# A mixture-of-experts block: the rows of the next block gathered and turned inside the down pass, the combine cut in two, the next expert's counts read there too

## The chip, the cores and the metric

One core of a Trainium2 chip runs the whole kernel. The metric is the device time of one execution in microseconds (us); lower is better. TensorE multiplies matrices, VectorE (DVE in the profile) and ScalarE (ACT) do elementwise work and empty PSUM, GpSimd (POOL) does a few set-up steps, SyncE (SP) issues nearly all DMA transfers.

## The reference, cut to what matters

A residual block over 256 tokens of width 1024: a mixer sub-layer (attention and a gated MLP), then a sub-layer with 32 experts, of which each token goes to 4. Everything is float32. The change is in the second one:

```python
logits = xt @ w_router + b_router              # 256 x 32
top_v, top_i = lax.top_k(logits, 4)
gates = softmax(top_v)
def expert(x, e):                              # the tokens that chose e
    gu = x @ w_gate_up[e] + b_gate_up[e]       # 1024 -> 2048
    x_glu = minimum(gu[:, :1024], 7.0)
    x_lin = clip(gu[:, 1024:], -7.0, 7.0)
    act = x_glu * sigmoid(1.702 * x_glu) * (x_lin + 1)
    return act @ w_down[e] + b_down[e]         # 1024 -> 1024
out[token] += gate * expert(x, e)[row of token]
```

Every expert has 12 MB of weights (8 MB gate-up, 4 MB down), all 32 are read, 384 MB in all.

## The kernel before, in words

**Stages.** For about the first 240 us the kernel does the mixer sub-layer and the router; the expert loop follows until about 1155 us, then a last combine, a norm and the output.

**Blocks.** The tokens of an expert are cut into blocks of at most 64 (`TB`). A block with at most 32 tokens runs in a *narrow* form (`m` = 32, each matmul 128x256 output, four column tiles), others in the *wide* form (`m` = 64, 128x512 output, two column tiles). In this run there are 37 blocks, 23 narrow and 14 wide, so five experts have two blocks. `tabs` holds, for each place in the order of experts, the number of blocks, the number of wide ones, and the expert. The first four places are experts 0 to 3; the others are ordered by load so that each four have one of the heaviest.

**One block on TensorE** (`block_of`, L1490): gather the block's rows by a matmul of a 0/1 selection `sel` with the normed tokens `h_sb` into PSUM bank `TOKS` (L1503); add the gate-up bias by small matmuls (L1512); turn the gathered rows by transposes (L1518); gate-up matmuls over eight `k` (L1539); combine the block *before* this one into the four output banks `po`, 4 matmuls (L1484); turn the activations in two halves (L1525); turn the gate-weighted selection `selg` (L1552); down matmuls over eight `k` (L1568). Between these, VectorE copies the gathered rows (L1085), does the clamped SwiGLU (L1091 to L1098) and builds `sel` and `selg` for the next block (L1103, L1107); ScalarE copies the turned rows `hgT` (L720), does the sigmoid (L723), copies the turned activations (L727), the turned selection (L730) and the block's result `y_sb` (L733 wide, L737 to L739 narrow). At an expert's start each engine loads that expert's counts from `tabs` into registers (L1580 and L1581 on TensorE, L1125 on VectorE, L714 on ScalarE).

**Transfers.** SP waits and issues them in one order (L453 to L478). The gate-up weights have two slots of 8 MB, each loaded in four parts of 2 MB; the low half of the down weights has two slots of 2 MB; the high half (`dhi`, 2 MB) has only one. During the last block of an expert, SP waits for these signals of TensorE:

```python
sp.wait_ge(s_gfree, total * 3)       # gate-up k = 0, 1 done: load part 0 of the expert after next
sp.wait_ge(s_gfree, total * 3 + 1)   # k = 2, 3 done: part 1
sp.wait_ge(s_dhi_free, total)        # down pass: six of eight k done (n == 5): dhi of the next expert
sp.wait_ge(s_y, total)               # down pass done: its second part, then parts 2, 3 and dlo
```

So between the first of these and the third only 4 MB are issued, and TensorE must come from the start of gate-up to near the end of the down pass.

**The end.** After the loop TensorE combines the last block (signal `s_fin`), ScalarE loads the table for the square root (L751) and squares (L755, L758), VectorE scales with `gain2`, which comes by a last DMA (L481).

## Time and profile before

| | |
|---|---|
| three runs | 1187.77, 1191.23, 1194.48 us; median 1191.23 |
| the profiled execution: time, and span from first to last instruction | 1186.76 us, 1184.5 us |
| busy share of the span | TensorE matmul 87%, weight load 42%, DVE 25%, ACT 15%, POOL 3% |
| DMA | 464.91 MB, mean 392 GB/s over the span |
| mean granted TensorE clock | 0.938 |
| longest waits of SP's queue | 353.8 us for L1568 (62 times), 222.9 us for L1539 (27 times) |

"PE" is TensorE's matmul row and "PEld" its weight loads; a clock of 1.00 is 2.4 GHz and 0.50 is 1.2 GHz. The trace lists each float32 matmul of the program as two (so a gather of 4 is x8, a narrow down pass x64, a wide one x32). Matmuls of different tiles overlap, so their busy times are not additive and the length of a group is read from where it starts and where the next begins. "issue" in the chain of waits is time in which TensorE waited for nothing that the profile shows. The transfer of an expert is issued long before it lands (a gate-up part has a median of 27.7 us from issue to landing), so SP waiting is no loss in itself: a loss is time in which no DMA engine moves anything.

### The profile page before, as it was taken

The numbers are of one execution on the slowest core, as the hardware profiler recorded it, in microseconds if no ns is written. First come the engines' busy times: TensorE is split into PE (matmuls) and PEld (weight loads), VectorE is DVE, ScalarE is ACT, GpSimd is POOL, SyncE is SP. The second block draws the span as 40 slices with busy tenths as digits, with TensorE's granted clock in tenths as the row PEclk, the third lists the DMA queues.
The fourth block names the chain that finished last, engine by engine and source line by source line (L and its number), as shares of the span: only waits on it lengthen the run. The fifth ranks groups of instructions, "written<-read, shape, count | busy, mean of one in ns | idle before, by whom it ended". The sixth has DMA issues, their size and how long they took to land.

```text
span 1184.5 us, 21565 instructions
## 1 busy us (share of the span) xinstructions
PE 1029.1 (87%) x8299; PEld 502.1 (42%) x8301; DVE 294.9 (25%) x813; ACT 179.7 (15%) x453; POOL 31.6 (3%) x54
## 2 busy tenths in 40 slices
PE   4999999977786999899989998999898989696966
PEld 4847887443342343334333433343334333232323
DVE  4636664241110121111211221112112211111112
ACT  3213340221110111101111111111111111010012
POOL 1001002110000000000000000000000000000000
PEclk9999999978897999899989998999899989898988
DMA  9899825989999979999999999999999999999996
GB/s 351 321 385 380 338 103 226 422 347 417 424 426 423 411 307 425 424 425 396 427 424 425 425 425 427 425 415 425 425 428 411 426 425 424 425 427 427 426 424 261
DMA packets 61484, 464.91 MB, mean 392 GB/s; under 512 B 5900, under 2 KB 10060, under 8 KB 28568
## 3 DMA queue, kind: packets, MB, share of 16 engines
q1 hardware_dynamic: 60736, 462.47, 94.6%
q0 software_dynamic: 336, 1.07, 0.3%
q10 hardware_dynamic: 392, 1.09, 0.2%
q8 instruction: 14, 0.23, 0.1%
q14 instruction: 6, 0.05, 0.0%
HBM read 462.50 MB, written 2.11 MB: 392 GB/s over the span
## 4 chain that ended last, share of the span: by engine, by line
PE 64%; DMA 23%; DVE 5%; issue 4%; ACT 2%; SPq 2%; DVEq 0%; POOL 0%; ACTq 0%
PE pp L1539 23%; DMA arena<-in_w_down_dram 20%; PE pp L1568 13%; PE pp L1325 5%; PE pp L1503 5%; PE pp L1247 2%; PE pp L1338 2%; PE po L1400 2%; PE pp L1257 2%; PE pp L1512 2%; PE po L1484 2%; DMA gain<-gain_dram 2%; DMA arena<-in_w_ada_dram 1%; PE pp L1518 1%; ACT work L720 1%
## 5 line engine op out<-in xcount | busy, mean ns | idle before, releaser
L1539 PE MATMUL pp<-arena,work 128*32 128x256 f32 (+1 forms) x3840 | 379.0, 449 | 20.1 <-ACT work L720 20.1
L1539 PEld LDWEIGHTS pp<-arena,work 128*32 128x32 f32 (+1 forms) x3840 | 168.3, 118 | 214.9 <-issue 131.3
L1568 PE MATMUL pp<-arena,work 128*32 128x256 f32 (+1 forms) x1920 | 200.2, 462 | 54.6 <-DMA arena<-in_w_down_dram 54.6
L1568 PEld LDWEIGHTS pp<-arena,work 128*32 128x32 f32 (+1 forms) x1920 | 77.1, 122 | 157.3 <-issue 67.9
L1091 DVE TENSOR_SCALAR work<-pp 128x128 f32<-128x128 f32 (+1 forms) x74 | 25.0, 338 | 410.2 <-PE pp L1539 410.2
L1503 PE MATMUL pp<-h_sb,work 128*32 128x256 f32 (+1 forms) x480 | 70.0, 514 | 41.9 <-issue 37.5
L723 ACT ACTIVATE work<-work 128x128 f32<-128x128 f32 (+1 forms) x74 | 25.9, 350 | 407.9 <-DVE work L1091 407.9
L1085 DVE COPY work<-pp 128x256 f32<-128x256 f32 (+1 forms) x37 | 19.5, 526 | 250.0 <-PE pp L1503 250.0
L1484 PE MATMUL po<-work 64*128 64x512 f32 x304 | 75.5, 615 | 1.2 <-ACT work L739 1.2
L1503 PEld LDWEIGHTS pp<-h_sb,work 128*32 128x32 f32 (+1 forms) x480 | 22.5, 129 | 84.9 <-issue 79.5
L1325 PE MATMUL pp<-arena 128*128 128x256 f32 x256 | 57.1, 382 | 0.0
L804 DVE SCALAR_TENSOR_TENSOR h_sb<-arena,small,h_sb 128x1024 f32<-128x1024 f32 x38 | 49.5, 1303 | 11.5 <-DMA arena<-in_w_ada_dram 10.3
L1325 PEld LDWEIGHTS pp<-arena 128*128 128x128 f32 x256 | 48.1, 190 | 8.1 <-issue 1.8
L1247 PE MATMUL pp<-arena 128*128 128x256 f32 x192 | 43.7, 390 | 0.3 <-DVE small L865 0.3
L1484 PEld LDWEIGHTS po<-work 64*128 64x128 f32 x304 | 26.2, 186 | 41.0 <-issue 39.2
L1247 PEld LDWEIGHTS pp<-arena 128*128 128x128 f32 x192 | 37.5, 196 | 6.2 <-issue 0.5
L1103 DVE TENSOR_SCALAR work<-iota,rank 128x64 f32 x74 | 15.5, 252 | 96.2 <-issue 91.3
L1107 DVE TENSOR_SCALAR work<-iota,rank,gate_tab 128x64 f32 x148 | 36.2, 309 | 0.0
L720 ACT COPY work<-pp 128x256 f32<-128x256 f32 (+1 forms) x37 | 16.7, 453 | 127.8 <-PE pp L1518 127.8
L1512 PE MATMUL pp<-bgu,pick 4*32 4x256 f32 (+1 forms) x480 | 34.4, 489 | 0.0
L737 ACT COPY work<-pp 128x256 f32<-128x256 f32 x23 | 8.6, 372 | 145.5 <-PE pp L1568 145.5
L1338 PE MATMUL pp<-arena 128*128 128x256 f32 x128 | 28.5, 381 | 0.0
(224 smaller groups left out, 622.7 us busy)
## 6 DMA issues: line engine op xcount, KB each, us to landing
arena<-in_w_gate_up_dram SPq DMA_DIRECT2D x128, 2048.0 KB, 27.7
arena<-in_w_down_dram SPq DMA_DIRECT2D x32, 2048.0 KB, 33.3
arena<-in_w_down_dram SPq DMA_DIRECT2D x64, 1024.0 KB, 20.1
arena<-in_w_ada_dram SPq DMA_DIRECT2D x11, 2048.0 KB, 14.0
arena<-in_w_in_dram SPq DMA_DIRECT2D x4, 2048.0 KB, 19.2
arena<-in_w_gate_dram SPq DMA_DIRECT2D x4, 2048.0 KB, 13.0
arena<-in_w_out_dram SPq DMA_DIRECT2D x2, 2048.0 KB, 10.6
arena<-in_w_ada_dram SPq DMA_DIRECT2D x2, 1024.0 KB, 13.3
```

Of the source, the lines that this page charges most:

```text
L720: a.copy(hgT[:, 0:w], pp[:, TURN, 0:w]).then_inc(s_turned, 1)
L723: a.activation(sig[:, hh, 0:w // 2], glu[:, hh, 0:w // 2], ACT.Sigmoid, scale=ALPHA).then_inc(s_sig, 1)
L804: ins = v.scalar_tensor_tensor(out=acc[:, n % 2, :], in0=page_k(pg, k), scalar=c_act[:, kk:kk + 1], in1=acc[:, n % 2, :], op0=ALU.mult, op ...
L1107: ins = v.tensor_scalar(selg[:, t, c, :], places, rank[:, t, e], gate_tab[:, t, e], ALU.is_equal, ALU.mult)
L1247: mm = t_.matmul(ps[:, i * TOK:(i + 1) * TOK], page_k(pg, k)[:, m * P:(m + 1) * P], hT[:, k, :], start=(k == 0), stop=(k == KD - 1))
L1325: mm = t_.matmul(ps[:, i * TOK:(i + 1) * TOK], page_k(pg, k)[:, m * P:(m + 1) * P], hT[:, k, :], start=(k == 0), stop=(k == KD - 1))
L1338: mm = t_.matmul(branch_bank(m)[:, half * TOK:(half + 1) * TOK], page_k(page_of(name), k)[:, m * P:(m + 1) * P], src[:, k, :], start=(k == 0),
L1484: mm = t_.matmul(po[:, 2 * t + j, :], selgT[j * TB:(j + 1) * TB, t, :], y_sb[j * TB:(j + 1) * TB, :], start=False, stop=last, skip_group_c ...
L1503: mm = t_.matmul(pp[j * m:(j + 1) * m, TOKS, 0:w], sel[:, t, 0:m], h_sb[:, t, j * w:(j + 1) * w], start=(t == 0), stop=(t == TT - 1))
L1512: t_.matmul(pp[j * m:(j + 1) * m, UP[hh], 0:w].rearrange("p (s f) -> p s f", s=2), pick[rows, r, 0:m], bgu[rows, :, cols], start=True, sto ...
L1539: mm = t_.matmul(pp[j * m:(j + 1) * m, UP[hh], 0:w].rearrange("p (s f) -> p s f", s=2), hgT[:, at:at + m], gu_w[slot][:, k, :, r * PAIR:(r ...
L1568: mm = t_.matmul(pp[j * m:(j + 1) * m, UP[0], 0:w], actT[:, at:at + m], wd[:, j * w:(j + 1) * w], start=(n == 0), stop=(n == KD - 1))
```

## The change

The gather of a block's rows (4 matmuls of the wide form, 64 columns of weights and 512 of rows, for narrow blocks too) and their turning move out of the block into the one before: the gather stands in the down pass before its fifth `k` (n == 4), the turning behind its last matmul. For block 1 both stand ahead of the loop. Of the combine's 4 matmuls two are done at the head of the block and two where all four were. The bias matmuls follow the half of the combine. VectorE builds `sel` and `selg` for the next block and copies its gathered rows at the end of each block, with the expert number loaded at the block's start; ScalarE copies the turned rows after `y_sb`. TensorE loads the next place's counts inside the down pass, before the gather. Before the loop VectorE computes `rank` and the first `sel` ahead of the counts. The cut diff:

```diff
@@ ScalarE
+            act.wait_ge(s_turn, 1)
+            a.copy(hgT, pp[:, TURN, :]).then_inc(s_turned, 1)
...
-                    act.wait_ge(s_turn, it)
-                    a.copy(hgT[:, 0:w], pp[:, TURN, 0:w]).then_inc(s_turned, 1)
...
                     if m == TB:
                         a.copy(y_sb, pp[:, UP[0], :]).then_inc(s_ysb, 1)
+                        act.wait_ge(s_turn, it + 1)
+                        a.copy(hgT, pp[:, TURN, :]).then_inc(s_turned, 1)
                         return
...
@@ VectorE
+            first = slice(0, 1)
+            select_rows(iota[:, 0:TB], first)
             counts = pp[:, 2, COUNT:COUNT + NEXP].rearrange("p (e a) -> p e a", a=1).to_broadcast([P, NEXP, 8])
...
+            take_rows(1, UP[1])
+            select_gates(iota[:, 0:TB], first)
...
-                dve.wait_ge(s_hg, it)
-                v.tensor_copy(hg[:, 0:w], pp[:, TOKS, 0:w]).then_inc(s_hgs, 1)
...
-                    dve.wait_ge(s_selT, it)
-                    select(iota[:, bass.ds(b * TB, TB)], e)
+                    past = dve.snap((b + 1) // nb, min_val=0, max_val=1)
+                    next_b = dve.snap((b + 1) % nb, min_val=0, max_val=NBLK - 1)
+                    next_n = dve.snap((past + n) % NEXP, min_val=0, max_val=NEXP - 1)
+                    next_e = dve.value_load(tabs[0:1, 2, bass.ds(next_n, 1)], min_val=0, max_val=NEXP - 1)
                     with dve.If(b < wide):
                         block_of(TB, it, halves)
                     with dve.Else():
                         block_of(NARROW, it, halves)
+                    dve.wait_ge(s_selT, it + 1)
+                    select_rows(iota[:, bass.ds(next_b * TB, TB)], bass.ds(next_e, 1))
+                    select_gates(iota[:, bass.ds(next_b * TB, TB)], bass.ds(next_e, 1))
+                    take_rows(it + 1, TOKS)
...
@@ TensorE
+            def gather(it, bank):
+                pe.wait_ge(s_sel, it)
                 for t in range(TT):
                     for j in range(2):
+                        mm = t_.matmul(pp[j * TB:(j + 1) * TB, bank, :], sel[:, t, :], h_sb[:, t, j * 512:(j + 1) * 512],
+                                       start=(t == 0), stop=(t == TT - 1))
+                mm.then_inc(s_hg, 1)
+
+            def turn_rows(it):
+                pe.wait_ge(s_hgs, it)
+                for i in range(4):
+                    mm = t_.transpose(pp[:, TURN, i * P:(i + 1) * P],
+                                      hg[:, i // 2 * PAIR + i % 2:(i // 2 + 1) * PAIR:2], ident[:])
+                mm.then_inc(s_turn, 1)
+
+            gather(1, UP[1])
+            pe.wait_ge(s_ysb, 2)
+            turn_rows(1)
+            pe.wait_ge(s_bd, 32)
+            pe.wait_ge(s_nblk, 1)
+            pe.wait_ge(s_tabs, 1)
...
                 pe.wait_ge(s_bgu[slot], landed * 2)
-                pe.wait_ge(s_sel, it)
-                for t in range(TT):
+                combine(it, ((0, 0), (0, 1)))
+                for hh in range(2):
                     for j in range(tiles):
-                        if (t, j) == (TT - 1, tiles - 1):
-                            pe.wait_ge(s_ysb, it + 1)
-                        mm = t_.matmul(pp[j * m:(j + 1) * m, TOKS, 0:w], sel[:, t, 0:m],
-                                       h_sb[:, t, j * w:(j + 1) * w], start=(t == 0), stop=(t == TT - 1))
-                mm.then_inc(s_hg, 1)
...
-                pe.wait_ge(s_hgs, it)
-                for i in range(q):
-                    mm = t_.transpose(pp[:, TURN, i * P:(i + 1) * P],
-                                      hg[:, i // 2 * PAIR + i % 2:(i // 2 + 1) * PAIR:2], ident[:])
-                mm.then_inc(s_turn, 1)
...
-                combine(it)
+                combine(it, ((1, 0), (1, 1)))
...
                 for n, k in enumerate(order):
+                    if n == 2:
+                        pe.wait_ge(s_aTev, halves[1])
+                    if n == 4:
+                        next_place()
+                        pe.wait_ge(s_selTev, it)
+                        gather(it + 1, TOKS)
                     if k in (4, 6):
                         pe.wait_ge(s_dhi[k // 2 - 2], dhi_landed)
-                    if n == 2:
-                        pe.wait_ge(s_aTev, halves[1])
-                    if n == KD - 1:
-                        pe.wait_ge(s_selTev, it)
...
                 mm.then_inc(s_y, 1)
+                turn_rows(it + 1)
...
-                    nb = pe.value_load(nblk_i[0:1, bass.ds(i * 2 + slot, 1)], min_val=1, max_val=NBLK)
-                    wide = pe.value_load(wide_i[0:1, bass.ds(i * 2 + slot, 1)], min_val=0, max_val=NBLK)
+                    nb = pe.snap(next_nb, min_val=1, max_val=NBLK)
+                    wide = pe.snap(next_wide, min_val=0, max_val=NBLK)
+
+                    def next_place():
+                        place = pe.snap((i * 2 + (slot + 1)) % NEXP, min_val=0, max_val=NEXP - 1)
+                        pe.reg_mov(next_nb, pe.value_load(nblk_i[0:1, bass.ds(place, 1)], min_val=1, max_val=NBLK))
+                        pe.reg_mov(next_wide, pe.value_load(wide_i[0:1, bass.ds(place, 1)], min_val=0, max_val=NBLK))
```

## Rows read from the trace of the kernel before

**Rows 1.** The page's slices: GB/s moved in each fortieth of the span.
```profile
GB/s 351 321 385 380 338 103 226 422 347 417 424 426 423 411 307 425 424 425 396 427 424 425 425 425 427 425 415 425 425 428 411 426 425 424 425 427 427 426 424 261
```

**Rows 2.** Windows: busy us per engine (PE, PEld, DVE, ACT, POOL), clock, DMA share, GB/s.
```profile
257.00:271.00 14.00, 11.20 (x164) 6.04 (x156) 5.32 (x24) 2.52 (x8) 0.00 (x0) 1.00 0.91 354
419.00:428.00 9.00, 8.84 (x51) 3.43 (x52) 1.96 (x8) 1.47 (x4) 0.00 (x0) 1.00 0.11 27
536.00:549.00 13.00, 11.18 (x164) 6.00 (x160) 3.37 (x14) 2.52 (x8) 0.00 (x0) 1.00 0.94 357
...
248.00:255.00 7.00, 5.77 (x58) 2.23 (x62) 1.73 (x7) 0.37 (x1) 0.00 (x0) 0.50 0.99 411
```

**Rows 3.** Chain of waits: a wide block's down pass, then two narrow blocks.
```profile
640.71 7.02 PE pp L1568 x32
...
650.55 7.51 PE pp L1539 x126
658.05 1.92 PE po L1484 x8
...
661.02 3.59 PE pp L1568 x64
664.62 1.59 issue
...
667.27 0.61 PE pp L1512 x16
...
668.79 3.36 PE pp L1539 x52
```

**Rows 4.** TensorE's sequencer at the down pass's fifth k: count, ns, first and last start.
```profile
L1560 PEldq FUSED_REGOPS  x1: 37/37/37, 661.4 to 661.4; - x1
```

**Rows 5.** TensorE's loads of the first count at one expert's start, the same columns.
```profile
L1580 PEldq TENSOR_LOAD <-tabs x1: 300/300/300, 682.0 to 682.0; - x1
```

**Rows 6.** TensorE's loads of the second count there, the same columns.
```profile
L1581 PEldq TENSOR_LOAD <-tabs x1: 301/301/301, 682.7 to 682.7; - x1
```

**Rows 7.** Timeline: a gather of the wide form.
```profile
684.13 1.94 PE L1503 MATMUL pp<-h_sb,work 128*64 128x512 f32 x8 [1.28 <-issue]
```

**Rows 8.** Timeline: ScalarE's first of three like copies of a narrow block's result.
```profile
664.68 0.37 ACT L737 COPY work<-pp 128x256 f32<-128x256 f32 x1 [3.25 <-PE pp L1568]
```

**Rows 9.** Groups by line and form: ScalarE's copy of 128x512 (busy us, mean ns).
```profile
L733 ACT COPY work<-pp 128x512 f32<-128x512 f32 x14 | 8.2, 585 | 93.4 <-PE pp L1568 93.4
```

**Rows 10.** Chain of waits: between the two wide blocks of one expert.
```profile
392.14 7.02 PE pp L1568 x32
...
400.91 1.02 PE pp L1512 x8
...
403.28 13.12 PE pp L1539 x60
```

**Rows 11.** Chain of waits: from a late DMA landing to the heavy expert's gate-up.
```profile
616.04 1.13 issue
617.17 3.68 PE pp L1503 x8
...
623.51 2.79 PE pp L1539 x11
```

**Rows 12.** Timeline of VectorE before the loop: the gate table.
```profile
243.33 0.39 DVE L1051 TENSOR_SCALAR gate_tab<-work,small 128x32 f32<-128x32 f32 x2
```

**Rows 13.** Timeline of TensorE: block 1's gather and gate-up.
```profile
248.77 1.94 PE L1503 MATMUL pp<-h_sb,work 128*32 128x256 f32 x16 [4.39 <-DVE work L1103]
...
252.84 9.05 PE L1539 MATMUL pp<-arena,work 128*32 128x256 f32 x128 [0.46 <-ACT work L720]
```

**Rows 14.** Timeline of ScalarE at the end: table load, first square.
```profile
1174.23 1.28 ACT L751 ACT_TABLE_LOAD   x1
1175.52 0.60 ACT L755 ACTIVATE h_sb<-po 128x512 f32<-128x512 f32 x1
```

**Rows 15.** Chain of waits at the end: the last DMA before the output.
```profile
1155.11 20.50 DMA gain<-gain_dram
```

More of the change, by code:

```diff
@@ L739, in block_of @@
                     a.copy(y_sb[2 * m:3 * m, w:2 * w], pp[3 * m:P, UP[0], 0:w]).then_inc(s_ysb, 1)
+                    act.wait_ge(s_turn, it + 1)
+                    a.copy(hgT, pp[:, TURN, :]).then_inc(s_turned, 1)
                 with act.Fori(0, nb) as b:
@@ L1098, in block_of, with blocks @@
                     v.tensor_tensor(x_sig, x_lin, x_sig, ALU.mult).then_inc(s_actv, 1)
-            def select(places, e):
-                dve.wait_ge(s_tabs, 1)
-                for t in range(TT):
-                    ins = v.tensor_scalar(sel[:, t, :], places, rank[:, t, e], None, ALU.is_equal)
-                ins.then_inc(s_sel, 1)
-                for t in range(TT):
-                    for c in range(2):
-                        ins = v.tensor_scalar(selg[:, t, c, :], places, rank[:, t, e], gate_tab[:, t, e], ALU.is_equal,
-                                              ALU.mult)
-                ins.then_inc(s_selg, 1)
-            def blocks(nb, wide, e):
+            def blocks(nb, wide, n):
                 with dve.Fori(0, nb) as b:
@@ L1144, in _ @@
             with dve.Fori(1, NEXP) as n:
-                nb, wide, e = place_of(bass.ds(n, 1))
-                blocks(nb, wide, bass.ds(e, 1))
+                nb, wide = place_of(bass.ds(n, 1))
+                blocks(nb, wide, n)
             dve.wait_ge(s_x1b, 16)
@@ L1534, in block_of @@
                             mm.then_inc(s_gfree, 1)
-                    at = (k % q) * P + (k // q) * m
+                    at = (k % 4) * P + (k // 4) * TB
                     for hh in range(2):
@@ L1594, in _ @@
             pe.reg_add(item, item, 1)
-            combine(pe.snap(item, min_val=1, max_val=NEXP * NBLK + 1), last=True)
+            combine(pe.snap(item, min_val=1, max_val=NEXP * NBLK + 1), ((0, 0), (0, 1), (1, 0), (1, 1)), last=True)
 _INS = ["x", "c", "w_ada", "b_ada", "g_pre_mix", "g_post_mix", "w_in", "rel_bias", "sgu_ln_g", "sgu_ln_b",
```

51 lines of the change are left out of this document (31 added, 20 removed).

## The prediction

> **What bounds the kernel now.** I read the slices of the page first. From the tenth slice on nearly all stand at 424 to 428 GB/s [rows 1]: the 384 MB of expert weights are streamed at the full rate, so TensorE's own work costs nothing there. What costs is time in which the DMA engines stand still. I take 427 GB/s as full and read the windows around the slices that fall short [rows 2]. From 257 to 271 us 354 GB/s moved, so 14 x (1 - 354/427) = 2.4 us are lost; from 419 to 428 us 8.4 us; from 536 to 549 us 2.1 us. These two are the first and second expert with two blocks; the others fall into the slices of 415, 411 and 411 GB/s (651, 770 and 888 us on), that is 0.8 to 1.1 us each over 29.6 us [rows 1].
>
> Each of these losses ends when SP is let past the down pass's signal `s_dhi_free`. SP has issued only 4 MB (some 10 us) since the first k of gate-up, and if nothing older is queued the stream dries up until TensorE is six k into the down pass. So of TensorE only two lengths count. One is from the last DMA it waited for to `s_dhi_free` of a heavy expert's last block: five times. The other is the same length in block 1. To these comes the tail behind the last down pass. Whatever is saved or lost in other blocks is covered by the queue.
>
> **Part by part.** All in us; minus is a gain.
>
> *The gather in the down pass.* In a narrow block it took little, but it now has the wide form, 1.94 at full clock [rows 7]. It stands between the halves of the down pass, ahead of `s_dhi_free`: +1.94 in every block. Its inputs are no wait: `sel` needs VectorE about 0.5 behind the turned selection, and half the pass is 1.8 narrow or 3.5 wide [rows 3].
>
> *The counts loaded there.* TensorE's sequencer executes register loads itself, and matmuls behind them wait. One starts at 682.0, the next at 682.7, each 0.3 with its register work to some 0.75 [rows 5, 6]: 1.5 for both, and I add 0.2 for the new place number. In a narrow block the sequencer stands at the fifth k at 661.4 to 661.5, 0.45 after the pass began at 661.02; it would be free at 663.2, while the array has finished half of 3.59 at 662.8 [rows 3, 4]. A bubble of about 0.5. In a wide block half of 7.02 is longer than the 2.2: no bubble. Bounds: 0, if it all hides, and 2.0, if the new address costs a further 1.5 (as much again as both loads).
> The Trainium skill (Advanced Engine Details and Errata, Engine Queue Depths and Sequencer Loop) gives TensorE a queue of 64 and says that instructions are queued while earlier ones wait; by that the loads would hide wholly. It is weighed below as a rival.
>
> *The head of the block.* Before, from the end of a narrow down pass (664.62) to gate-up (668.79) went 4.17 [rows 3], with loads, gather, bias, copy, turn, copy in a row. After, the result's copies end 1.2 after the pass (three in a row of 0.37 from 664.68 on [rows 8]), half a combine is 1.92/2 = 0.96, bias 0.61 [rows 3]: 2.8, and `hgT` is ready earlier. Gain 1.3. Behind a wide block of the same expert the copy is 0.585 [rows 9]: a wide block follows after 0.1 + 0.6 + 0.96 + 1.02 = 2.7 in place of 4.12 (399.16 to 403.28, bias included [rows 10]), gain 1.4; a narrow one after 2.3 in place of 2.82 (647.73 to 650.55 [rows 3]), gain 0.5. After a DMA wait the clock is low and the head dear: 616.04 to 623.51 is 7.47, of it 3.68 the gather [rows 11], which now falls into the wait ahead of the landing. After: 1.2 + 1.9 (half combine at half clock) + about 1.5 bias = 4.6, gain 2.85.
>
> *The combine split.* VectorE and ScalarE set the pace behind gate-up. In a narrow block the first turn can come sooner: gain 0.45 of the 1.92 [rows 3]. In a wide one the second activation half is late anyway: nothing.
>
> *VectorE and ScalarE* have long idle stretches under gate-up (13.1 wide, 7.5 narrow [rows 3, 10]) for the loads, `selg` and copies. If that cover were gone, one block's moved work there is under 3.
>
> **The sum, by place.**
> Start. The gate table is done at 243.7 [rows 12]; rank and `sel` take 1 more, so the gather starts near 244.7 instead of 248.77, but at half clock [rows 2] takes 3.7, then copy and turn 1.8 (from 250.71 to 252.84 the old chain did these and the bias [rows 13]), half combine 1.9, bias 1.0: gate-up at 253.1 against 252.84. TensorE is at work 4 earlier, so the clock probably rises earlier, which takes 0.7 from this chain and 1.0 from gate-up. Bounds +0.4 and -2.5; I take -1.0.
> Block 1 (narrow) to `s_dhi_free`: 1.94 + 0.5 - 0.45 = +2.0.
> Wide, wide (the 8.4 loss): head -2.8, -1.4, gathers +3.9: -0.3.
> Wide, narrow, three times: -2.85 - 0.5 - 0.45 + 3.9 + 0.5 = +0.6; the one near 500 us, whose clock stayed low longest, +1.4; less 0.3 where the loss before was smallest: +2.9.
> Tail. Last block: 2.0 as block 1, and 0.35 for half a combine at low clock in its head. Then a useless `hgT` copy of 0.6 stands ahead of the table load of 1.28 that ends at 1175.5 [rows 14]. Less 0.2, since the squares waited for the last DMA, landed at 1175.6 [rows 15]: +2.75.
> Sum: -1.0 + 2.0 - 0.3 + 2.9 + 2.75 = **+6.35**. The profiled execution took 1186.76 (span 1184.5), so 1193.1, 0.53% more. It was a little faster than the shown median of 1191.23; against that the same share gives **1197.5**.
>
> **Rivals.**
> *Slower by more (1203).* The place number's remainder and the waits stretch the bubble to 2.0, in wide blocks too by 0.5, or code is fetched late inside the pass. Six narrow blocks x 1.5 = 9, less what DMA waits cover, some 6 more than forecast. For: the loads are the only stop of the sequencer in a pass. Against: nothing shows a costlier register instruction.
> *Everything is covered (1193.5).* The bubble is nothing, as the queue rule would have it (6 x 0.5 = 3.0 less) and the start gains 1.5 more: 6.35 - 4.5 = +1.9. For: the sequencer does run ahead of the array. Against: it had only 0.45 to 1.3 of lead at this place [rows 3, 4].
> *Faster (1184).* The mechanism is TensorE's clock at heavy heads and at the start. It was 0.50 from 248 to 255 [rows 2], and the gather of 3.68 against 1.94 shows the low level at 617 [rows 7, 11]. If the gather, run in the DMA wait, kept it at full, a head would cost 1.2 + 0.96 + 1.02 = 3.2 and gain another 1.4, and gate-up near 500 some 2; five heads 9, the start 2.5 more, tail 0.4, in all 6.35 - 11.9 = -5.5, with the bubble gone too -8. It decides once heads average 1.3 less than forecast. Against: the gather sits at the beginning of the wait, not at its end, and the head after it is less dense than before. The Trainium skill (TensorE: Matmul & The Clock Gate, HAM oscillation) says that waits for DMA between bursts throttle the clock again; the low clock behind the wait agrees, and by it the gather ahead of the wait saves nothing.
> *The change does less than it says:* losses are fixed by DMA alone, and only the tail counts: +2.75, 1194. Against: 27 GB/s for nine microseconds [rows 2] while TensorE works through a wide block.
>
> **How the numbers follow.** 0.5%, or 6 us, is about what a measurement of this kernel can tell from no change. Forecast (+4 to +9) 0.50; slower by more 0.16; all covered or tail only 0.24; faster 0.10. The forecast lies on the bound, a little above: half of it counts as slower. With the larger rival: slower 0.45, with the covered cases same 0.45, faster 0.10. The range leaves out most of the faster case and the top of the other: 1190 to 1206, the bounds of start (1.5 either way), bubble (3 down, 6 up) and the runs' own spread of 3 taken together.
>
> **What would show it.** In the profile after: the gather x8 in 1.9 inside the down pass of narrow blocks; a gap of about 0.5 ahead of it there and none in wide blocks; narrow heads of 2.8; 257 to 271 us losing some 3.5 in place of 2.4; the 8.4 loss unchanged; windows at the other heavy experts losing 0.5 to 1.5 more each; first square at the end about 3 later behind the last down landing. I am wrong if gaps ahead of the gather are over 1.5 or none, if heads after a DMA wait still take 7, or if the clock there stays at full.

## The result and the profile after

| | before | after |
|---|---|---|
| median of 11 runs each, taken side by side | 1187.99 us (1185.65 to 1194.48) | 1192.05 us (1187.60 to 1196.63) |
| the profiled execution: time, span | 1186.76, 1184.5 | 1187.60, 1185.3 |
| mean granted TensorE clock there | 0.938 | 0.957 |

The ratio after to before is 1.0037, 95% interval 1.0021 to 1.0053: slower by 0.37%, some 4 us. The sign is the predicted one; 1197.5 was 5.4 us too high. The profiled execution of after is the fastest of its eleven, so the pair of traces shows 0.8 us of the 4.1.

The slices of GB/s after, as [rows 1]:

```profile
GB/s 350 322 385 377 339 105 227 414 329 402 425 425 425 424 308 425 425 425 426 425 425 425 424 425 427 425 417 425 425 425 416 425 425 425 426 425 426 425 427 246
```

The ninth slice, where the loop begins, fell from 347 to 329. The 19th, 396 before, is full now: a loss is gone. One of the windows of [rows 2] in the kernel after, with three wider ones:

```profile
248.00:255.00 7.00, 3.84 (x26) 1.29 (x24) 1.58 (x5) 0.58 (x1) 0.00 (x0) 0.71 0.95 389
...
255.00:280.00 25.00, 22.02 (x260) 9.78 (x256) 6.01 (x25) 3.16 (x9) 0.00 (x0) 0.84 0.86 343
412.00:434.00 22.00, 20.98 (x144) 7.95 (x144) 5.12 (x15) 2.91 (x7) 0.00 (x0) 1.00 0.66 268
534.00:556.00 22.00, 20.56 (x284) 9.91 (x276) 4.96 (x19) 3.47 (x10) 0.00 (x0) 1.00 1.01 426
```

Since the work now lies some microseconds later, a short window can cut a loss in two. The wide ones hold each loss whole. Those three of before:

```profile
255.00:280.00 25.00, 18.84 (x242) 9.24 (x238) 5.74 (x25) 2.90 (x9) 0.00 (x0) 0.84 0.96 385
412.00:434.00 22.00, 21.38 (x170) 8.46 (x170) 4.86 (x15) 2.81 (x7) 0.00 (x0) 1.00 0.65 267
534.00:556.00 22.00, 19.71 (x311) 10.68 (x302) 3.79 (x15) 2.90 (x9) 0.00 (x0) 1.00 0.98 385
```

With 427 GB/s as full, as in the prediction, 25 x (1 - 385/427) = 2.5 us were lost from 255 to 280 before, and 25 x (1 - 343/427) = 4.9 after. From 412 to 434 it is 8.2 both times. From 534 to 556 it is 2.2 before and nothing after. So the start of the loop lost 2.4 more, the wide-wide expert (the heavy one whose two blocks are both wide) is unchanged, and in this pair of executions the second heavy expert lost 2.1 less. The run before_spin below shows that this last difference need not come from the change.

The chain of waits after: block 1, then a heavy expert behind a late landing, a wide block's gather, a narrow block and the last one:

```profile
244.92 3.20 PE pp L1498 x8
...
248.98 0.72 PE pp L1505 x4
249.69 2.28 issue
251.97 2.08 PE po L1520 x4
254.05 1.03 PE pp L1539 x16
255.08 8.22 PE pp L1560 x120
...
620.76 13.05 PE pp L1560 x60
...
641.46 1.72 PE pp L1498 x8
643.18 3.43 PE pp L1591 x16
...
658.84 1.86 PE pp L1591 x32
660.71 0.35 issue
661.05 1.94 PE pp L1498 x8
...
667.84 4.20 PE pp L1560 x69
...
1167.46 1.93 PE pp L1591 x32
```

L1498 is the gather, L1505 the turning, L1520 the combine, L1539 the bias, L1560 gate-up, L1591 the down pass. Inside the loop it looks as forecast: a gather of 1.94 in the narrow pass behind a gap of 0.35, no gap in the wide one (643.18 follows 641.46 + 1.72), a narrow head of 3.0 (the pass ends at 664.84, gate-up starts at 667.84). Ahead of the loop it does not: behind the turning TensorE stands still for 2.28, and gate-up starts at 255.08 where it was 252.84 [rows 13]. The sequencer (the part of the engine that reads the instructions in order, "PEldq" here) shows what happens in that gap. These rows are the wait ahead of the turning (count, ns, first and last start) and the two loads of the first counts, which the source has behind it:

```profile
L1503 PEldq EVENT_SEMAPHORE  x1: 51/51/51, 248.9 to 248.9; - x1
L1603 PEldq TENSOR_LOAD <-tabs x1: 489/489/489, 249.4 to 249.4; - x1
...
L1604 PEldq TENSOR_LOAD <-tabs x1: 313/313/313, 250.3 to 250.3; - x1
```

The wait for the copied rows is here an instruction of the sequencer itself. It ran at 248.9, right after VectorE's copy of the rows had ended at 248.84, and the loads behind it only at 249.4 and 250.3, though VectorE had written their inputs by 246.1. Nothing was left for the array (the matmul unit) then but four transposes, 0.72 us. In the kernel before they ran at 245.7 and 246.7, and were over when the first gather's inputs came at 248.77.

The end (timeline of ScalarE, as [rows 14]):

```profile
1174.77 0.58 ACT L744 COPY work<-pp 128x512 f32<-128x512 f32 x1
1175.37 1.28 ACT L756 ACT_TABLE_LOAD   x1
1176.67 0.60 ACT L760 ACTIVATE h_sb<-po 128x512 f32<-128x512 f32 x1
```

The copy of rows that nobody needs (0.58) stands ahead of the table load, as forecast. The first square is 1.15 later than before.

### The profile page after: what moved, and what is told of

It reads as the page before. It is cut to its first block, busy times and chain, and to the rows that moved or that the text cites. A ratio compares the mean times of both kernels' runs of the same rounds, so it can differ in the third digit from the quotient of the medians.

```text
span 1185.3 us, 21465 instructions
## 1 busy us (share of the span) xinstructions
PE 1048.0 (88%) x8174; PEld 498.4 (42%) x8175; DVE 303.1 (26%) x820; ACT 184.6 (16%) x454; POOL 31.4 (3%) x54
## 4 chain that ended last, share of the span: by engine, by line
PE 58%; DMA 30%; DVE 6%; issue 2%; ACT 2%; SPq 2%; POOL 0%; DVEq 0%; ACTq 0%
DMA arena<-in_w_down_dram 28%; PE pp L1560 19%; PE pp L1591 12%; PE pp L1342 5%; PE pp L1498 4%; PE po L1520 3%; PE pp L1264 2%; PE pp L1355 2%; PE po L1417 2%; PE pp L1274 2%; PE pp L1539 2%; DVE work L1117 1%; DMA arena<-in_w_ada_dram 1%; DVE work L1114 1%; DVE work L1115 1%
## 5 line engine op out<-in xcount | busy, mean ns | idle before, releaser
L1560 PE MATMUL pp<-arena,work 128*32 128x256 f32 (+1 forms) x3840 | 373.6, 444 | 0.0
L1591 PE MATMUL pp<-arena,work 128*32 128x256 f32 (+1 forms) x1920 | 205.3, 461 | 54.3 <-DMA arena<-in_w_down_dram 54.3
L1560 PEld LDWEIGHTS pp<-arena,work 128*32 128x32 f32 (+1 forms) x3840 | 162.0, 117 | 210.1 <-issue 148.8
L1591 PEld LDWEIGHTS pp<-arena,work 128*32 128x32 f32 (+1 forms) x1920 | 74.5, 121 | 171.7 <-DMA arena<-in_w_down_dram 80.2
L1520 PE MATMUL po<-work 64*128 64x512 f32 x304 | 91.6, 682 | 18.4 <-ACT work L742 9.6
L1498 PE MATMUL pp<-h_sb,work 128*64 128x512 f32 x304 | 74.2, 607 | 8.1 <-issue 7.7
L1342 PE MATMUL pp<-arena 128*128 128x256 f32 x256 | 57.1, 382 | 0.0
L1081 DVE COPY work<-pp 128x512 f32<-128x512 f32 x38 | 26.3, 691 | 118.4 <-PE pp L1498 118.4
L1546 PE MATMUL pp<-ident,work 128*128 128x128 f32 x102 | 29.2, 331 | 26.6 <-DVE work L1121 26.6
L1520 PEld LDWEIGHTS po<-work 64*128 64x128 f32 x304 | 24.4, 196 | 48.7 <-issue 31.0
L1264 PE MATMUL pp<-arena 128*128 128x256 f32 x192 | 43.8, 391 | 0.3 <-DVE small L870 0.3
L1498 PEld LDWEIGHTS pp<-h_sb,work 128*64 128x64 f32 x304 | 22.1, 138 | 47.9 <-issue 47.9
L1546 PEld LDWEIGHTS pp<-ident,work 128*128 128x128 f32 x102 | 15.1, 175 | 61.7 <-DVE work L1121 61.7
L1075 DVE TENSOR_SCALAR work<-iota,rank,gate_tab 128x64 f32 (+1 forms) x152 | 37.2, 309 | 0.0
L1505 PEld LDWEIGHTS pp<-ident,work 128*128 128x128 f32 x152 | 22.1, 209 | 25.6 <-issue 25.6
L1539 PE MATMUL pp<-bgu,pick 4*32 4x256 f32 (+1 forms) x480 | 32.1, 468 | 0.0
## 6 DMA issues: line engine op xcount, KB each, us to landing
arena<-in_w_down_dram SPq DMA_DIRECT2D x64, 1024.0 KB, 20.5
arena<-in_w_out_dram SPq DMA_DIRECT2D x2, 2048.0 KB, 10.6
```

The source lines that it names most:

```text
L1075: ins = v.tensor_scalar(selg[:, t, c, :], places, rank[:, t, e], gate_tab[:, t, e], ALU.is_equal, ALU.mult)
L1081: v.tensor_copy(hg, pp[:, bank, :]).then_inc(s_hgs, 1)
L1264: mm = t_.matmul(ps[:, i * TOK:(i + 1) * TOK], page_k(pg, k)[:, m * P:(m + 1) * P], hT[:, k, :], start=(k == 0), stop=(k == KD - 1))
L1342: mm = t_.matmul(ps[:, i * TOK:(i + 1) * TOK], page_k(pg, k)[:, m * P:(m + 1) * P], hT[:, k, :], start=(k == 0), stop=(k == KD - 1))
L1498: mm = t_.matmul(pp[j * TB:(j + 1) * TB, bank, :], sel[:, t, :], h_sb[:, t, j * 512:(j + 1) * 512], start=(t == 0), stop=(t == TT - 1))
L1520: mm = t_.matmul(po[:, 2 * t + j, :], selgT[j * TB:(j + 1) * TB, t, :], y_sb[j * TB:(j + 1) * TB, :], start=False, stop=last, skip_group_c ...
```

## Experiments

Eleven measurements in three groups, of nine new kernels, the kernel after (again) and a repeat (start_spin_2). All of a group ran on one chip with the kernel before beside them; ratios are to that. Each has 12 runs, double_gather 6 and head_combine 9; before has 35, 35 and 20. The ratio is taken over all the runs, so it is not quite the quotient of the two medians.

| kernel | median us (lowest, highest) | before | ratio, 95% interval | lost 255 to 280 us |
|---|---|---|---|---|
| again | 1191.36 (1185.95, 1196.03) | 1187.39 | 1.0025 [1.0006, 1.0043] | 6.3 |
| start_loads | 1186.78 (1184.44, 1191.82) | 1187.39 | 0.9983 [0.9971, 0.9995] | 2.5 |
| late_gather | 1190.15 (1187.95, 1192.08) | 1187.39 | 1.0015 [1.0003, 1.0026] | 6.1 |
| spin | 1187.87 (1184.99, 1190.78) | 1187.39 | 0.9999 [0.9985, 1.0013] | 4.4 |
| start_spin | 1185.17 (1181.84, 1191.82) | 1188.44 | 0.9986 [0.9967, 1.0005] | 0.1 |
| before_spin | 1187.27 (1184.55, 1189.61) | 1188.44 | 0.9995 [0.9982, 1.0007] | 1.9 |
| head_loads | 1190.23 (1186.52, 1192.92) | 1188.44 | 1.0013 [1.0000, 1.0026] | 6.1 |
| late_start_spin | 1185.71 (1182.87, 1188.66) | 1188.44 | 0.9974 [0.9961, 0.9988] | 2.0 |
| start_spin_2 | 1187.16 (1183.20, 1192.68) | 1187.64 | 0.9994 [0.9976, 1.0012] | 2.9 |
| double_gather | 1202.06 (1198.60, 1205.18) | 1187.64 | 1.0115 [1.0095, 1.0136] | 4.6 |
| head_combine | 1191.94 (1188.66, 1196.35) | 1187.64 | 1.0032 [1.0014, 1.0050] | 2.1 |

The last column is 25 x (1 - GB/s / 427) from each one's profiled execution, a single one.

**again**: the kernel after, unaltered.

> The changed kernel once more, unaltered, as the yardstick of the three beside it. The first profile of it (1187.6 us) is the fastest of its 11 runs, whose median is 1192.05, and its low-clock stretches sum to 104 us against 149 us before. Theory 'places': the change costs some 3.7 us at the start and block 1 and little elsewhere; ratio 1.002 to 1.005. Rival 'clock': the time follows how many low-clock stretches a run draws; then this profile, if its time is near 1192, has one or two stretches of 7 to 14 us more than the first, and a DMA loss of 1 to 3 us behind them at a heavy expert.

The difference repeats: 1.0025 here, 1.0037 there, the intervals overlap. Its trace starts as the first did: gather 3.69, issue 1.82, gate-up at 255.18. The case that the rival 'clock' asked for, a profiled execution near 1192, did not come: this one took 1188.63, so it does not decide between the two theories.

**start_loads**: the first counts are loaded before the wait of the turning.

```diff
             gather(1, UP[1])
+            pe.wait_ge(s_nblk, 1)
+            pe.reg_mov(next_nb, pe.value_load(nblk_i[0:1, 0:1], ...))
+            pe.reg_mov(next_wide, pe.value_load(wide_i[0:1, 0:1], ...))
             pe.wait_ge(s_ysb, 2)
             turn_rows(1)
             pe.wait_ge(s_bd, 32)
-            pe.wait_ge(s_nblk, 1)
             pe.wait_ge(s_tabs, 1)
...
-            pe.reg_mov(next_nb, pe.value_load(nblk_i[0:1, 0:1], ...))
-            pe.reg_mov(next_wide, pe.value_load(wide_i[0:1, 0:1], ...))
```

> Alone moved: the two counts of the first expert are loaded between block 1's gather and its turning, while the gather runs, and not behind the turning. Theory 'places' (TensorE stands 2.3 us after the turning for these loads, and the DMA stream waits for block 1): gate-up of block 1 starts 1.5 to 2.0 us earlier than 255.1, and the median falls by 1.5 to 2 us against the unaltered one. Rival 'clock': the start comes earlier but the clock falls at it all the same, and the median moves by under 0.7 us.

The chain of waits at its start:

```profile
245.42 3.70 PE pp L1498 x8
...
249.97 1.10 PE pp L1505 x4
251.08 0.12 issue
...
253.95 7.02 PE pp L1563 x116
```

The loads now run at 246.6 and 247.6, under the gather, and 0.12 of idle time is left in place of 2.28 (1.82 in again). Gate-up follows the gather's start by 8.5 us in place of 10.2 to 10.6, as foretold, and from 255 to 280 us 2.5 us are lost, as in the kernel before. The median is 4.6 below again, where 1.5 to 2 were expected, and just below before, with an interval that excludes 1. This one place carries the slowdown. That it is worth more than its gap fits the length of block 1: from the gather's start to the down pass it takes 18.4 us here (245.42 to 263.79) and 21.2 in after and 22.8 in again; 1.7 to 2.2 of the difference is the gap, and 1.2 to 2.4 is gate-up, which ran in 7.02 here and in 8.22 and 9.43 there, partly at the low clock. The lost stream is 2.4 to 3.8 less. The profiled execution itself is the slowest of its twelve (1191.82): it lost 10.4 us from 412 to 434 and 2.9 from 640 to 680, where again lost 7.8 and 0.2. So the 4.6 stands on the twelve runs and not on a pair of traces.

The loss from 255 to 280 us follows the length from the gather's start to the down pass. In the versions that differ from after only ahead of the down pass it is 15.8 us with 0.1 lost (start_spin), 18.4 with 2.5 (start_loads), 18.9 with 2.9 (start_spin_2), 20.4 with 4.4 (spin), 21.2 with 4.9 (after) and 22.8 with 6.3 (again): nearly one for one.

**late_gather**: the loads and the gather stand ahead of the seventh k, behind `s_dhi_free`.

```diff
-                    if n == 4:
+                    if n == 6:
                         next_place()
```

> Alone moved: the gather of the next block and the loads with it stand before the seventh k of the down pass, behind the signal that frees the high half of the down weights, and not before the fifth. Theory 'places': the signal comes 1.9 (wide) to 2.3 us (narrow) earlier in block 1 and in each heavy expert's last block; block 1 gives 2.2 us, the wide-wide expert (8.2 us lost) 1.9, the others what they lose, 0 to 1; in all 4 to 5 us, so 1187 to 1188, about level with the kernel before. Rival 'clock' or 'tail': the place of the signal decides nothing measurable; under 1 us.

The gather of block 1's pass now starts at 271.00, behind the signal. SP issues the first half of `dhi` at 270.81, 2.0 earlier than in again, though gate-up began 0.8 later. But the median is only 1.2 below again, where 4 to 5 were expected, and the two intervals overlap. One reason stands in the order of SP's waits: only 1 MB, some 2.5 us of stream at 427 GB/s, is let past by `s_dhi_free`. The second half and all behind it wait for `s_y`, the end of the pass, which the move of the gather does not bring nearer: the second half goes out at 274.13 here and at 273.63 in again. The start of this kernel still has its gap (issue 1.89) and loses 6.1. So the place of the gather is a small term, not the one that carries the result.

**spin**: filler matmuls ahead of the loop hold the clock up for the first gather, nothing else is changed. `spin(n)` is the kernel's own helper, n matmuls of bf16 data into a bank not yet in use.

```diff
             route(1)
+            spin(8)
             pe.wait_ge(s_chosen, TT)
...
             mm.then_inc(s_gT, 1)
+            spin(1)
             pe.wait_ge(s_h2, 2 * TT)
```

> Added: nine bfloat16 matmuls on data nobody reads, while TensorE waits for the router ahead of block 1 (eight before the rank matmuls, one before the gather). Theory 'clock': they keep the clock at full through the gather, which then takes 1.9 in place of 3.2, the half combine 1.1 in place of 2.1 and the bias 0.6 in place of 1.0, so gate-up of block 1 starts 2.5 to 3.5 us earlier than 255.1 and the median falls by as much. Rival 'places': the clock falls anyway behind the turning, while the loads run; the gather gains its 1.3 and no more. If the nine delay the rank, it shows as a gather later than 244.9.

Chain of waits at its start:

```profile
243.41 1.95 PE pp L1500 x8
...
246.94 2.26 issue
249.20 2.08 PE po L1522 x4
...
252.31 8.65 PE pp L1562 x120
```

The gather took 1.95 in place of 3.20 to 3.69, but the gap of 2.26 stayed and behind it the clock was low again (a half combine of 2.08). From the end of ScalarE's table load (240.57) gate-up starts after 11.7 us, where after needs 13.0 and again 13.4: the gather gains its 1.3 and little more, as the rival 'places' had it. Yet the median is 3.5 below again, of the 4.0 that again is above before. The lost stream (4.4 in place of 4.9 and 6.3) explains 0.5 to 1.9 of that; where the rest comes from is not shown. As measured, taking away either the loads' gap or the low clock of the gather brings the kernel back to about before.

**start_spin** is start_loads and spin together; **before_spin** puts the same filler into the kernel before.

> The changed kernel with both edits at the start: the first counts loaded during block 1's gather, and the nine unread bfloat16 matmuls ahead of it. Each alone gave a median of 1186.78 and 1187.87 against 1191.36. Theory 'places': the two act on different pieces of the chain (1.9 us of standing for loads; gather at 1.9 in place of 3.7), so gate-up of block 1 starts some 6.5 to 7 us behind the gather's start in place of 10.1 to 10.5, and the median is 1184 to 1186. Rival 'the runs' spread': both single gains were luck of the draw above 2 us each; then the median stays at 1187 or over.

> The kernel before with the clock edit alone: eight unread bfloat16 matmuls ahead of the rank matmuls and fourteen while TensorE waits for the first selection. Asks whether what the clock gives at the start has to do with the change at all. Theory 'places': gather to gate-up of block 1 takes 2.5 to 3 us in place of 4.1 and gate-up itself starts at full clock, in all 2 to 3 us off the median of before (1187.4), 1184.5 to 1185.5; the change then has no hand in it. Rival: the low clock costs only the changed kernel, since only its wide gather stands there; then before moves by under 1 us.

```diff
 # the kernel before
             route(1)
+            spin(8)
...
             mm.then_inc(s_gT, 1)
+            spin(14)
             pe.wait_ge(s_bd, 32)
```

start_spin's gate-up begins 8.8 us after the end of ScalarE's table load ahead of the gate table (241.84 to 250.64), where before needs 10.9 and after 13.0. With the loads gone the gap is 0.51 where spin has 2.26, so the loads are some 1.75 of it. The stream loses 0.1 in the window:

```profile
255.00:280.00 25.00, 20.50 (x248) 9.05 (x244) 6.00 (x25) 3.16 (x9) 0.00 (x0) 0.86 1.02 425
...
345.00:412.00 67.00, 55.21 (x312) 18.79 (x304) 9.93 (x32) 6.37 (x17) 0.00 (x0) 0.92 1.01 427
412.00:434.00 22.00, 20.98 (x206) 9.28 (x206) 4.89 (x17) 2.85 (x8) 0.00 (x0) 1.00 0.69 275
```

The median lies where it was expected, but the interval of the ratio (0.9967 to 1.0005) takes in 1, and four of the twelve runs took 1189 to 1192 us: see start_spin_2.

In before_spin the filler shortens the way from gather to gate-up to 2.8 (4.1 before), as expected, but the 2 to 3 us off the median did not come: 1.2 by the medians, 0.6 by the ratio, whose interval takes in 1. So the low clock at the start cost the kernel before little or nothing that these runs can tell. Its trace shows something else. Its code in the loop is that of the kernel before, and yet the loss of 2.1 to 2.2 us at the second heavy expert is not there, and another stands at the third:

```profile
534.00:556.00 22.00, 19.55 (x248) 9.10 (x248) 5.39 (x22) 3.62 (x13) 0.00 (x0) 0.92 1.02 429
640.00:680.00 40.00, 36.85 (x457) 18.14 (x460) 7.78 (x31) 6.26 (x19) 0.00 (x0) 1.00 0.96 390
```

From 490 to 510 us its clock was 1.00, where before had 0.66; then it was low for 17.1 us from 609.1 on, and 40 x (1 - 390/427) = 3.5 us are lost from 640 to 680. One and the same loop thus loses nothing or 2 to 3.5 us at a heavy expert, and in these two executions the loss stands where the clock was low just ahead of it.

**head_loads**: the counts are loaded at each expert's start, as before, not in the down pass.

```diff
                     if n == 4:
-                        next_place()
                         pe.wait_ge(s_selTev, it)
...
-                    nb = pe.snap(next_nb, ...)
-                    wide = pe.snap(next_wide, ...)
+                    nb = pe.value_load(nblk_i[0:1, bass.ds(i * 2 + slot, 1)], ...)
+                    wide = pe.value_load(wide_i[0:1, bass.ds(i * 2 + slot, 1)], ...)
```

> The changed kernel with one part undone: TensorE loads the counts at the expert's start again and not inside the down pass. The gap ahead of a narrow block's gather, 0.35 us, goes; the loads (1.5 to 1.7) come back at the head, where turning and the result's copies cover about 1.2 of them. Theory 'places': within 0.7 us of the unaltered one (1191.4 to 1192.1). Rival of the prediction ('the loads in the pass cost 2 us'): 3 to 6 us faster. Rival 'the loads at the head were the gain': heads of heavy experts are 1.5 longer and the median is 3 us or more higher.

Chain of waits, the block of 661 us:

```profile
664.97 0.78 issue
665.75 1.13 PE po L1520 x4
```

The gap of 0.35 ahead of the gather is gone (the first half of the pass ends at 660.04 and the gather starts there) and one of 0.78 stands at the head instead: that is what the move of the loads is worth. The first expert's loads still stand behind the turning (issue 1.75, loss 6.1), and the time lies with again and late_gather: 1.0013 beside 1.0025, with intervals that overlap. These runs cannot tell this kernel from the kernel after.

**late_start_spin**: late_gather, start_loads and spin together.

> All three edits together: gather before the seventh k, first counts loaded during the first gather, nine unread matmuls. Late gather alone gave 1190.15 against 1191.36. Theory 'places': block 1 frees the high half 2 us sooner, the loss near 420 to 430 us shrinks by 1.9 us; against start_spin another 1 to 3 us less, 1182 to 1184. Rival: the late gather's gain is taken back, since VectorE's copy of the rows (0.7) and the turning now stand behind the pass in narrow blocks; then it equals start_spin within 1 us.

0.9974 with an interval below 1: of all versions this one beats both kernels most clearly, 2.7 us against before. Against start_spin it is no gain (1185.71 beside 1185.17), where 1 to 3 us were expected: the rival held. The loss from 412 to 434 us did not shrink either, 9.3 in the profiled execution where after has 8.2.

**start_spin_2**: start_spin once more.

> The same kernel as start_spin once more, as the base of the two runs beside it. If the start is the only term that was wrong in sign, it stays 2 to 4 us below the kernel before, gate-up starts 8.8 us behind ScalarE's table load in place of 13.0, and the DMA engines lose under 1 us between 255 and 280 us. If its lead was chance, its median is back within 1 us of the kernel before.

0.9994 after 0.9986: parity with before, or about 1 us under it. The median is 0.5 below before's, inside the 1 us that the expectation named as the sign that the first lead was chance; a lead of 2 to 4 us did not repeat. Gate-up starts 9.4 behind the table load's end (240.55 to 249.95), not 8.8, and 2.9 were lost in the window where under 1 was expected: the clock was 0.54 from 248 to 255 where start_spin had 1.00, and gate-up took 9.53 in place of 6.98. Its profiled execution took 1191.48, start_spin's 1182.38: the same kernel, 9.1 us apart. The windows of the slower one:

```profile
255.00:280.00 25.00, 21.85 (x260) 9.67 (x256) 6.01 (x25) 3.16 (x9) 0.00 (x0) 0.86 0.94 378
...
345.00:412.00 67.00, 55.57 (x308) 18.79 (x300) 9.17 (x30) 6.07 (x16) 0.00 (x0) 0.85 0.99 412
412.00:434.00 22.00, 20.97 (x134) 7.72 (x134) 5.12 (x15) 2.91 (x7) 0.00 (x0) 1.00 0.56 221
```

At 425, 427 and 275 GB/s the other lost 0.1, 0 and 7.8, this one 2.9, 2.4 and 10.6: 8 of the 9.1 us. They go together with the clock. It was 0.74 from 365 to 390 us, at the head and gate-up of the first heavy expert, where the other had 0.99 (chain of waits):

```profile
372.59 15.87 PE pp L1565 x60
```

The next gate-up of the same form in this run, at full clock, takes 13.05. What differs between these two executions is where the low stretches fall, not the work.

**double_gather**: start_spin with the gather of the down pass done twice.

```diff
-                for t in range(TT):
+                for t in list(range(TT)) * times:
                     for j in range(2):
...
-                        gather(it + 1, TOKS)
+                        gather(it + 1, TOKS, times=2)
```

> start_spin with the gather in the down pass done twice (8 matmuls of 64x512 in place of 4), 1.94 us more in each of 37 blocks, 72 us of TensorE time in all. By the prediction's account every gather ahead of s_dhi_free in block 1, in both blocks of the five heavy experts and in the last block is on the path: 12 x 1.94 = 23 us slower than start_spin. Rival: the first block of a heavy expert runs into the landing of its own down weights, so that one gather per heavy expert counts: 7 x 1.94 = 13.6 us. Second rival: at the four heavy experts with a narrow second block nothing counts, since the queue still holds transfers when the signal comes; then block 1, the wide-wide expert (one or two) and the last block count: 5.8 to 7.8 us.

14.9 us over start_spin_2. A doubled gather takes 3.65 in a narrow pass and 3.43 in a wide one, a single one 1.94 and 1.72:

```profile
669.76 3.65 PE pp L1500 x16
```

So the second one adds 1.71 and not 1.94, 63 us of TensorE time in all. Windows:

```profile
412.00:434.00 22.00, 20.99 (x118) 7.35 (x118) 5.12 (x15) 2.91 (x7) 0.00 (x0) 1.00 0.55 219
...
534.00:556.00 22.00, 20.54 (x264) 9.23 (x265) 4.06 (x15) 3.48 (x10) 0.00 (x0) 1.00 0.88 362
...
640.00:680.00 40.00, 37.54 (x362) 15.80 (x362) 9.18 (x30) 6.07 (x16) 0.00 (x0) 1.00 0.92 383
760.00:800.00 40.00, 37.54 (x334) 15.46 (x338) 9.17 (x30) 6.07 (x16) 0.00 (x0) 1.00 0.93 386
```

By 427 GB/s these are 10.7, 3.3, 4.1 and 3.8 us lost; start_spin_2 has 10.6, 0.1, 0.3 and 0.7 there, start_spin 7.8 in the first. From 850 to 980 us, around the fifth heavy expert, it is 4.6 (412 GB/s) beside 1.2 (423). So each of the four heavy experts with a narrow second block loses 3.1 to 3.8 more, which is both of its second gathers (2 x 1.71 = 3.4) and not one of them. There the account of the prediction holds: lengths up to `s_dhi_free` reach the time. The rival with one gather for each heavy expert has the total that lies nearest (13.6), but these windows speak against its mechanism; the second rival (nothing at four experts) is out. By the account 12 x 1.71 = 20.5 us were due and 14.9 came. What is missing is at the wide-wide expert, with 0.1 more from 412 on, and at block 1, with 1.7 more. But start_spin_2 had its low clock at just that wide-wide expert, and double_gather's mean granted clock is 0.977 where start_spin_2 has 0.955. How much a steadier clock gave back is not shown.

**head_combine**: start_spin with all four combine matmuls at the head.

```diff
-                combine(it, ((0, 0), (0, 1)))
+                combine(it, ((0, 0), (0, 1), (1, 0), (1, 1)))
...
-                combine(it, ((1, 0), (1, 1)))
```

> start_spin with all four combine matmuls at the head of the block and none behind gate-up. If the prediction's term for the split is right (0.45 us gained behind gate-up in a narrow block, 0.96 us paid at the head, 1.9 at low clock), the second half costs 0.96 more at the head and gives at most 0.45 back behind gate-up: 0.5 us at each of block 1, five heavy experts and the last block, 3 to 4 us slower than start_spin. Rival: the half behind gate-up lies wholly in the wait for VectorE and ScalarE while the head is exposed only in block 1 and the last: 1 to 2 us slower. Second rival: a head without exposed length, no difference within 1 us.

4.8 us slower than start_spin_2, at or a little above the first theory's 3 to 4. In block 1 the combine at the head takes 3.26 at a clock partly low, where start_spin's half took 1.13 and start_spin_2's 1.26 (chain of waits at its start):

```profile
247.31 3.26 PE po L1525 x8
...
251.51 6.98 PE pp L1565 x120
```

The half behind gate-up is nearly free: from gate-up's end to the down pass block 1 takes 2.8 us here without it and 2.8 in start_spin with it, since TensorE waits for VectorE and ScalarE there. The same half at the head is on the path. In this pair that shows at the heavy experts, where 1.5 us are lost from 534 to 556 and 2.8 from 640 to 680 (start_spin_2: 0.1 and 0.3), and not at block 1, which loses 2.1 where start_spin_2 loses 2.9. So the second half is well placed behind gate-up. Whether the first half would be better there too was not tried in the changed kernel, so nothing here shows what the split itself is worth.

## Why the prediction was right and wrong

**The base: 3.2 us.** The sum was +6.35 on the profiled 1186.76, that is 1193.1, and I laid its share on the three runs' median of 1191.23. With eleven runs before has 1187.99. The shown profiled execution stood nearer to the kernel's usual time than the median of three did; +6.35 on 1187.99 would have been 1194.3, still 2.3 above the measured 1192.05.

**The start: the step that failed.** Predicted -1.0, bounds +0.4 and -2.5; gate-up stood 2.2 later (255.08), by the table load's end 13.0 against 10.9. Of the prediction's pieces the earlier gather came (244.92, forecast 244.7), its low clock came (3.2 and 3.7), half combine and bias came (2.1 and 1.0). What was missing is the gap of 2.28, most of it the loads of the first expert's counts (2.26 with them in spin, 0.51 without them in start_spin). I had priced exactly these loads at 1.5 in the down pass [rows 5, 6], and counted them nowhere at the start, where the change puts a wait of the sequencer in front of them and leaves nothing on the array to cover them. With the loads moved (start_loads) 4.6 us went. My bound had no term for it. The remark that an earlier start of TensorE would lift the clock earlier was half right: from 248 to 255 us the clock was 0.71 in place of 0.50 [rows 2], but the gap ate the gain.

**Block 1 to the signal: the length about right, the path half seen.** +2.0 predicted. From gate-up's start to the signal before takes 15.0 (252.84 to about 267.8), after 16.4 (255.08 to 271.5): +1.4, of which 1.94 gather, 0.35 gap, -0.45 if the split gave what was forecast, and the rest a gate-up 0.4 shorter (8.62 to 8.22). But the prediction has each loss end at `s_dhi_free`, and at block 1 the stream runs dry twice. Windows of before, then after, then start_loads:

```profile
255.00:266.00 11.00, 10.75 (x148) 5.84 (x144) 4.01 (x18) 1.43 (x5) 0.00 (x0) 0.95 0.93 362
266.00:280.00 14.00, 8.09 (x102) 3.40 (x98) 1.73 (x7) 1.47 (x4) 0.00 (x0) 0.76 0.98 404
...
255.00:266.00 11.00, 10.45 (x144) 5.08 (x136) 2.06 (x8) 0.94 (x4) 0.00 (x0) 0.88 0.80 305
266.00:280.00 14.00, 11.56 (x118) 4.70 (x120) 3.95 (x17) 2.22 (x6) 0.00 (x0) 0.81 0.91 373
...
255.00:266.00 11.00, 10.10 (x152) 4.89 (x145) 3.36 (x14) 1.48 (x5) 0.00 (x0) 1.00 1.01 404
266.00:280.00 14.00, 11.89 (x140) 5.28 (x144) 2.64 (x11) 1.69 (x4) 0.00 (x0) 0.88 0.90 368
```

The first of the two dry stretches ends with gate-up's own first signal (`s_gfree`), behind which SP issues the next transfers, at 257.80, 259.66 and 257.30. It costs 1.7, 3.1 and 0.6 us. Only the second waits for `s_dhi_free`: 0.8, 1.8 and 1.9. So the late start is paid at the first signal, where start_loads wins it back, and the longer way behind gate-up at the second, about 1.1 where 2.0 was forecast.

**In the loop: the prices right, the sum not.** The gather 1.94, the bubble 0.35 (0.5 forecast), none in wide blocks, the narrow head 3.0 (2.8), the head after a DMA wait 4.2 (4.6, before 7.47 [rows 11]): nearly all as priced, and the expert of 614 us has its length unchanged where +0.6 stood. Yet +2.9 for the heavy experts did not appear: the losses there went from 2.2, 0.1 and 0.8 to 0.1, 0.1 and 0.7 (from 534, 640 and 760 us on), and stayed at 1.2 from 850 to 980. Two more steps failed. The expert near 500 us was given +1.4; before, its clock had been low for 13.7 us from 495.1 on, after it was not, and its loss of 2.1 was gone. I took that loss for a property of the kernel, but before_spin, with the same loop, does not have it either: it went with where the clock was low in the one execution shown. And I misread the slices: the one of 651 us, where I put a loss of 0.8 to 1.1, is the 23rd and stands at 425; the three that fall short are the 14th, 27th and 31st (385, 770 and 888 us on) [rows 1]. So one of the heavy experts lost nothing before, and a longer way to the signal could have been free there up to a margin. double_gather shows that the margin is small: two gathers more per expert, 3.4 us, cost 3.2, 3.8 and 3.1 there. The change itself needs none, since its head gives back what its gathers take. The +0.6 per expert is made up by the bubble (0.35 for 0.5) and by a head that gained 3.3 (7.47 to 4.2) where 2.85 was forecast.

**The 8.4 loss unchanged: right** (8.2 to 8.2), head savings and gathers cancelling as summed.

**The tail: sized right, partly given back.** +2.75 predicted. From the last down pass's start to the first square before takes 6.2 (1169.35 to 1175.52), after 9.2 (1167.46 to 1176.67), +3.0: gather, gap and the useless copy. (The first square did not wait for the last DMA, as I had it: it began at 1175.52, and the DMA landed at 1175.61 [rows 14, 15].) But gate-up of the last block took 7.46 in place of 9.02, whose clock was low, and the pass started 1.9 sooner, right at the landing of its own weights (the chain after, 1167.46). Counted from the landing at 1152 us, +0.7 is left in this pair.

**The sum.** Predicted start and block 1 +1.0, heavy experts +2.6, tail +2.75. Shown: start and block 1 +2.4 to +3.8 of lost stream, and 4.6 in the time when the gap was taken out; the rest together about nothing (start_loads stands at 0.9983). The direction came out as forecast by luck: the slowdown sits in the term that I had as a gain, and the terms that carried the forecast, heavy experts and tail, show little or nothing. The two errors had opposite signs. The number was too high because of the heavy experts, the tail and the base, and too low at the start.

**The rivals.** Everything covered, 1193.5, comes nearest in size, but not by its mechanism: there is a bubble, and the start lost. It rested on the queue rule of the Trainium skill (Advanced Engine Details and Errata, Engine Queue Depths and Sequencer Loop). In wide blocks the loads are hidden, and there the trace agrees; in narrow ones a gap of 0.35 shows, and there it does not (the page itself calls the depth complicated with tiling, and these matmuls are tiled). The same Sequencer Loop has engine instructions wait in the queue while others are read behind them. The rows of L1503 show a wait that is an instruction of the sequencer itself, with the loads behind it only after 248.9, so that rule does not cover this wait. The rival of a faster clock had a seed of truth: where the loss of 2.1 vanished at 534 us the clock had stayed up. That the change keeps it up there is not shown, as before_spin's was up too. Over the eleven runs of after time and mean granted clock go together with a correlation of -0.94, from 1187.60 at 0.957 to 1196.63 at 0.946. In the kernel before the tie is looser: -0.61 over the 35 runs beside again.

## What to carry to other kernels

Ask of each scalar load on a sequencer what wait the new order puts ahead of it. Here two loads behind a wait had nothing to hide them, and the same two ahead of it, under a gather, cost 0.12 of idle time; that move was worth 4.6 us. Where a change fits into the slack of a stream, double its work: here the second gather cost nearly its full length at four experts at which neither kernel lost much. A loss read from one execution may be a draw of the clock; look for it in a second one before you build a term on it. And lay a sum on the execution that it was read from, when the runs shown are three and spread by 6 us.

## What was not expected of the hardware

Two executions of the same kernel differed by 9.1 us, 8 of them in lost stream at places where TensorE's clock happened to be low in one and not in the other: a wide gate-up of 15.87 in place of 13.05 in the first heavy expert. The low clock came again right behind a gap of 2.26 us even though the gather ahead of it had run at the full one (1.95, then a half combine of 2.08 for 1.13). A register load at the start took 489 ns and the next 313, against 300 in the loop [rows 5]; with the register work around them TensorE stood still for 1.8 to 2.3 us, and for 0.5 in start_spin, where the loads had moved.
